# Tile 0 first: its norm, two query units and the scores of head 0 move into the merge block, and the choice of head 0 opens the expert block

## What is computed

```
merged = gates[:, :, 0, :] * conv_out + gates[:, :, 1, :] * attn_out
x = x + merged @ w_out[l]
h2 = rmsnorm(x, norm2_g[l])
x = x + peer_ffn(h2, peer_w_query[l], peer_sub_keys[l], peer_u[l], peer_v[l])

def peer_ffn(...):          # per token, for 8 heads
    q = (hc @ w_query)      # 8 heads x 2 halves x 128
    sc = einsum('thpd,pnd->thpn', q, sub_keys)      # 2 x 128 scores
    vals, idx = top_k(sc, 16)                       # 16 best of each half
    top_s, pos = top_k(cand, 16)                    # 16 best of their 256 sums
    gate = softmax(top_s)
    act = gelu(einsum('thkd,td->thk', expert_u[expert_idx], hc))
    return einsum('thk,thkd->td', gate * act, expert_v[expert_idx])
```

## Time and profile before

| what | value |
|---|---|
| median of 3 runs | 2574.63 us (2572.73 to 2579.84) |
| profiled execution, its own time | 2570.52 us |
| its span in the trace | 2568.7 us |
| mean granted PE clock | 0.976 of full speed |
| PE busy | 2220.0 us, 86% of the span |
| DVE busy | 1697.4 us, 66% |
| ACT busy | 866.9 us, 34% |
| POOL busy | 857.3 us, 33% |
| gathers (software queue) | 536.90 MB |
| plain transfers | 143.49 MB |

### The profile page before, as it was taken

One profiled execution on the slowest core, in us unless ns is written; L12 is line 12 of the kernel. 1 busy time (PEld: TensorE's weight loads), 2 busy tenths in 40 slices (PEclk: granted clock), 3 DMA queues, 4 the chain that ended last, 5 costly groups with the idle time before them and its releaser, 6 DMA issues. The chain is left out here.

```text
span 2568.7 us, 33318 instructions
## 1 busy us (share of the span) xinstructions
PE 2220.0 (86%) x11942; PEld 1394.2 (54%) x11942; DVE 1697.4 (66%) x3855; ACT 866.9 (34%) x1931; POOL 857.3 (33%) x649
## 2 busy tenths in 40 slices
PE   8998999889987788877777777777789999999999
PEld 7886667765442334333232222322267788776787
DVE  7998797347776778666776667667544644456553
ACT  4222762333232333322232223322234223246431
POOL 0001213355454355434434343333333211212243
PEclk9999999999999999999999999999999999989999
DMA  4232215279999999999999999999942212232253
GB/s 155 101 109 95 79 50 181 74 264 412 420 421 419 421 417 409 415 420 416 418 415 416 420 416 416 410 407 420 422 172 90 87 65 72 97 128 87 91 193 107
DMA packets 131075, 682.51 MB, mean 266 GB/s; under 512 B 13536, under 2 KB 23136, under 8 KB 65120
## 3 DMA queue, kind: packets, MB, share of 16 engines
q0 software_dynamic: 73728, 536.90, 50.6%
q1 hardware_dynamic: 57184, 143.49, 16.0%
HBM read 655.70 MB, written 24.64 MB: 265 GB/s over the span
## 5 line engine op out<-in xcount | busy, mean ns | idle before, releaser
L1681 PE MATMUL bank<-peer_uv,peer_diag 128*128 128x512 f32 x2048 | 967.3, 617 | 287.6 <-ACT peer_diag L1336 277.7
L1574 DVE SCALAR_TENSOR_TENSOR peer_uv<-peer_uv,early_h 128x1024 f32<-128x1024 f32 x512 | 644.5, 1270 | 381.3 <-DMA peer_uv<-in_peer_uv,peer_index 373.7
L1681 PEld LDWEIGHTS bank<-peer_uv,peer_diag 128*128 128x128 f32 x2048 | 383.3, 195 | 832.4 <-issue 828.9
L1373 POOL DMA_INDIRECT peer_uv<-in_peer_uv,peer_index x512 | 528.6, 1033 | 750.1 <-PE bank L1681 661.4
L229 POOL TENSOR_TENSOR weight_low<-weight_ring,weight_high 128x1024 fp32r<-128x1024 f32 x100 | 243.7, 2437 | 639.3 <-ACT weight_high L212 639.3
L155 PE MATMUL bank<-hT_high,weight_high 128*128 128x512 f32 (+2 forms) x952 | 399.0, 419 | 10.2 <-POOL weight_low L229 4.3
L157 PE MATMUL bank<-hT_high,weight_low 128*128 128x512 f32 (+2 forms) x984 | 380.9, 387 | 1.5 <-issue 1.5
L156 PE MATMUL bank<-hT_low,weight_high 128*128 128x512 f32 (+2 forms) x952 | 371.1, 390 | 0.0
L212 ACT ACTIVATE weight_high<-weight_ring 128x1024 fp32r<-128x1024 f32 x169 | 178.6, 1058 | 458.2 <-PE bank L157 436.8
L1331 ACT ACTIVATE peer_gelu<-peer_dots 128x2 f32<-128x2 f32 x256 | 52.1, 203 | 793.3 <-DVE peer_uv L1574 789.5
L1336 ACT ACTIVATE peer_diag<-const,peer_weight 128x128 f32<-128x128 f32 x512 | 177.5, 394 | 116.9 <-DVE peer_weight L1479 109.7
(11 more groups left out here) (422 smaller groups left out, 2748.6 us busy)
## 6 DMA issues: line engine op xcount, KB each, us to landing
weight_ring<-in_weights SPq DMA_DIRECT2D x171, 512.0 KB, 3.3
z_store<-fill_stage SPq DMA_DIRECT2D x70, 256.0 KB, 2.4
peer_uv<-in_peer_uv,peer_index POOLq DMA_INDIRECT x512
merge_z<-z_store SPq DMA_DIRECT2D x8, 768.0 KB, 6.2
merge_z<-z_store SPq DMA_DIRECT2D x12, 512.0 KB, 4.8
score_store<-peer_work SPq DMA_DIRECT2D x16, 192.0 KB
peer_sc<-score_store SPq DMA_DIRECT2D x24, 128.0 KB
swz<-z_store SPq DMA_DIRECT2D x1, 2560.0 KB, 9.6
```

The source lines that it names most:

```text
L1373: pool.indirect_dma_start(uv[:, p % SLOTS], None, peer_uv, bass.IndirectOffsetOnAxis(index[:, n % 2, p % TOPK:p % TOPK + 1], 0)).then_inc( ...
L1574: nc.vector.scalar_tensor_tensor(uv[:, p % SLOTS, 0:D], uv[:, p % SLOTS, 0:D], 1.0, h2[:, t], ALU.mult, ALU.mult, accum_out=dots[:, p % TO ...
L1681: mm = nc.tensor.matmul(bank[2 * (t % 2) + c][:], diag[:, p % SLOTS], uv[:, p % SLOTS, D + c * 512:D + (c + 1) * 512], start=(p % PICKS == ...
```

## The change

In the merge block w_out's last `k` takes the tiles in the order 0, 1, 2, 3. Behind it PE turns tile 0, computes the first two query units for tile 0 alone, and scores them; ACT and DVE make tile 0's high and low parts; ACT keeps the two queries and scores in `early_sc`, which the expert block uses as `sc`. In the expert block DVE starts with the choice of head 0 and its index, ahead of the low parts of h2; the turning, parts and the first two query units are done for tiles 1 to 3 alone. `EARLY` is 4: 40 query steps (four units, their scores, and half of the fifth unit) run ahead of the loop in place of 71. The loop takes 9 steps in four groups instead of 8. The choices of the later heads form one stream (`choices`) with four pieces a group: a head's choice starts when its scores are kept, and not within a fixed head. `MEM_AT` moves from 46 to 58.

```diff
+                pe.wait_ge(normed, 1)
+                for f in range(DT):
+                    nc.tensor.transpose(turned_at(f), xn[:, 0, f * P:(f + 1) * P], ident).then_inc(turned, 1)
+                for n in range(2):
+                    ring = w.wait(pe, q0 + n)
+                    pe.wait_ge(added, 4)
+                    for k in range(DT):
+                        if n == 0:
+                            pe.wait_ge(x_low, k + 1)
+                        mm = product(nc, bank[2 + n][:, 0:P], ring[:, k], hT[:, k, first], k == 0, k == DT - 1)
+                    mm.then_inc(queried, 1)
+                for n in range(2):
+                    pe.wait_ge(query_kept, n + 1)
+                    pe.wait_ge(added, 6)
+                    nc.tensor.matmul(bank[4 + n][:, 0:P], query[:, n], subkeys[:, n], start=True, stop=True
+                                     ).then_inc(scored, 1)
...
-EARLY = 8
+EARLY = 4
...
-STEPS = 2
+def steps_before(g):
+    return 9 * g // 4
+LOWS_BEFORE = {3: 1, 4: 1, 5: 2}
...
-                for n in range(2, EARLY - 2):
-                    w.low_part(pool, nc.gpsimd, u0 + n)
-                lows = EARLY - 2
+                lows = 2
                 for g, n, q, t in groups():
...
+                def may_choose(m, g):
+                    if m >= HEADS or g < GROUPS * (m - 2):
+                        return False
+                    return g > (keep_score_groups()[2 * m + 1] if m < PH else keep_score_groups()[-1] + 2)
+
+                def choices():
+                    for m in range(1, HEADS):
+                        while not may_choose(m, at[0]):
+                            yield
+                        yield from choose(m)
+                        while at[0] < GROUPS * (m - 1):
+                            yield
+                        publish(m)
+                        yield
+
+                for _ in choose(0):
+                    pass
+                publish(0)
                 for n, f in enumerate(TURN_ORDER):
                     dve.wait_ge(x_high, n + 1)
...
-                for _ in both(0):
-                    pass
                 dve.wait_ge(gained, TT)
+                at = [-1]
+                ahead = choices()
```

More of the change, by code:

```diff
@@ L955, in merge_first, with turned_at @@
             "ready", "warm_ready", "added", "squared", "mean_ready", "root_ready", "rstd_ready", "normed"))
-        u0 = first_unit("wo")
+        query = st.sb("query", [P, 2, P])
+        turned, x_high, x_low, queried, query_kept, scored = (st.sem(n) for n in (
+            "turned", "x_high", "x_low", "queried", "query_kept", "scored"))
+        u0, q0 = first_unit("wo"), first_unit("query")
         tiles = z_store.rearrange("(b f) p t -> f p b t", b=3)
+        first = slice(0, P)
+        def turned_at(f):
+            return bank[f // 4][:, f % 4 * P:(f % 4 + 1) * P]
         order = (2, 3, 0, 1)
@@ L982, in _ @@
                     pe.wait_ge(low_ready, k + 1)
-                    for t in order:
+                    for t in order if k < DT - 1 else range(TT):
                         for e in range(2):
@@ L1059, in _ @@
                 mean(0)
+                scale(0)
                 add(2)
-                scale(0)
                 mean(1)
                 add(3)
-                for i in range(1, TT):
-                    scale(i)
-                    if i + 1 < TT:
-                        mean(i + 1)
+                for f in range(DT):
+                    dve.wait_ge(x_high, f // 4 * 4 + 4)
+                    nc.vector.scalar_tensor_tensor(hT.low[:, f, first].bitcast(F32R), turned_at(f), norm2[:, f:f + 1],
+                                                   hT.high[:, f, first], ALU.mult, ALU.subtract).then_inc(x_low, 1)
+                for t in range(1, TT):
+                    scale(t)
+                    if t + 1 < TT:
+                        mean(t + 1)
 HEADS = TT * PH
@@ new lines, in score @@
+                def score(n):
+                    pe.wait_ge(query_kept, n + 1)
+                    if 2 <= n < 4:
+                        pe.wait_ge(score_kept, n - 1)
+                    elif n >= 4:
+                        pe.wait_ge(first_kept, n - 3)
+                    for t in range(1 if n < 2 else 0, TT):
+                        mm = nc.tensor.matmul(bank[6 + n % 2][:, t * P:(t + 1) * P], queryT[:, n % 2, t * P:(t + 1) * P],
+                                              subkeys[:, n % 2], start=True, stop=True)
+                    mm.then_inc(scored, 1)
@@ new lines, in queries @@
+                def queries():
+                    for n in range(QUERIES):
+                        ring = w.wait(pe, u0 + n)
+                        if n >= 2:
+                            pe.wait_ge(query_kept, n - 1)
+                        for i, k in enumerate(TURN_ORDER):
+                            if n == 0:
+                                pe.wait_ge(x_low, i + 1)
+                            if n and i == DT // 2:
+                                score(n - 1)
+                                yield
+                            mm = product(nc, bank[4 + n % 2][:, tokens(n)], ring[:, k], h2T[:, k, tokens(n)], i == 0, i == DT - 1)
+                            if i == DT - 1:
+                                mm.then_inc(w.done, 1)
@@ L1670, in _ @@
                 side = queries()
-                for _ in range(DT * EARLY + EARLY - 1):
+                for _ in range(PREFIX):
                     next(side)
@@ L1684, in _ @@
                     mm.then_inc(summed, 1)
-                    for _ in range(STEPS):
+                    for _ in range(steps_before(g), steps_before(g + 1)):
                         next(side, None)
```

192 lines of the change are left out of this document (94 added, 98 removed).

## The result

The changed kernel takes 2595.34 us (median of 5 runs, 2593.06 to 2598.49), the kernel before 2574.63: ratio 1.0078, 95% interval 1.0062 to 1.0094. It is 20.7 us slower, where I forecast 2573. The profiled execution is the median one: its own time 2595.34, its span 2593.5 us, 24.8 longer than the profiled one of before.

A forecast was written before the change was run, and what follows sets the result against it. The prediction took the gathers' transfers to bound the expert loop from its first gather on. Its terms, -26.0 + 6.0 + 5.2 + 5.0 + 8.5 = -1.3 us, applied to the median 2574.63, gave 2573, range 2559 to 2585.

The forecast's parts named there:

- A: From the merge block to the first gather: it goes out earlier, at 512.9 instead of 538.93, -26.0 us.
- B: From the first to the eleventh gather: the way gets longer, 40.7 us instead of 34.7, +6.0 us.
- C: Expert loop: loads of units 4 to 7 and their stored scores now lie among the gathers, +5.2 us.
- D: Expert loop, head 1: its index comes late, behind six groups instead of three, leaving transfers idle, +5.0 us.
- E: Expert loop, heads 2 to 6: their indices come late, 1.7 us lost five times, +8.5 us.
- the lead stays: Rival for the loop's late indices: they cost nothing at heads 2 to 6, 3.3 us at head 1; 2563, chance 0.33.
- costs twice: Rival for the loop's late indices: heads 2 to 6 lose 3.5 us each, head 1 6.8; 2584, chance 0.16.
- At no cost ... The later memory product: Expert loop: the later memory product fits into about 1.5 us a group free on PE, costing nothing.
- The sum's silent term: Behind the expert loop: everything was taken as unchanged, with no term in the sum.

The follow-up runs named there:

- e9: e6 with POOL's low parts of units 2 and 3 made before the third and fourth pairs of gathers: 2565.27 us.
- e12: e9 with the load of unit 5 ahead of the first score store on SP's queue: 2564.11 us.
- e11: e6 with the load of unit 5 ahead of the first score store on SP's queue: 2566.98 us.
- e5: The changed kernel with score loads ahead of the weight load and six choice pieces a group for tile 0's groups: 2568.05 us.
- e6: e5 with 80 more idle matmuls in the groups from 150 on: 2564.75 us.
- e13: e12 with ACT keeping the last score ahead of the loop behind group 0's diagonals: 2561.70 us.
- e14: e6 with ACT keeping the last score ahead of the loop behind group 0's diagonals: 2562.05 us.
- e1: The changed kernel with the loads of later heads' scores ahead of the weight load on SP's queue: 2582.99 us.
- e2: The changed kernel with six choice pieces a group instead of four for tile 0's groups: 2576.93 us.
- e3: The kernel before with 48 more idle matmuls in the groups from 150 on: 2582.11 us.
- e4: The changed kernel with 80 more idle matmuls in the groups from 150 on: 2585.24 us.
- e7: The kernel before with 128 more idle matmuls in the groups from 150 on: 2575.82 us.
- e8: The kernel before with 80 more idle matmuls in the groups from 150 on: 2574.88 us.

## Why the prediction was wrong, by its steps

Sizes are those of the profiled executions: 24.8 us longer is -24.5 (first gather) + 34.1 (loop) + 15.2 (rest).

**A, the first gather: -24.5, predicted -26.0.** The choice took 7.84 where I had 7.8; it began 1.4 us late (506.09, not 504.7). But this is the good case. In the twelve profiled kernels with the change in it the first gather goes out between 514.1 and 521.4. In e9, at 518.9, PE had the granted clock 0.50 from 506 to 514, the lower level of 1.2 GHz, and ACT waited 3.29 us for the second query where it was 0.85; PE had been partly idle just before (2.21 of 4 us busy in 498 to 502). But e12 had the same (2.22 of 4) and kept 0.98 of the clock in 506 to 514, so what decides it is open. The order of work makes PE wait for tile 0's norm and parts in short pieces, and then run the new product at half speed in some executions. I had that idling in B, not in A.

**B, the way to the eleventh gather: +8.5, predicted +6.0.** The size is near by luck in part, for the path was another. The wait for the load of unit 4, 1.8 us in my working, did not come: I had given that load 14.1 us, and it took 8.4. Two waits came that I had at nothing. PE's third unit ended 21.8 us behind the first gather (536.2) and not 18.8: POOL issued six gathers ahead of its low part, and PE's idle time and the lower clock behind it made that unit 3.7 us longer, of which 3.0 are left, as the two units before had ended 0.7 sooner than in my working. From there to the gather it took 1.3 us more than my working has without its 1.8, and 1.1 of them are the store's. So 3.0 - 1.8 + 1.3 = 2.5 too little. By the Trainium skill, "DMA: Bandwidth & Descriptors", section on queues, rings and completion order, an engine goes round between its queues by packets; by that these transfers would not wait for the gathers' backlog. Here the two loads and the store took 8.4, 15.0 and 9.2 us, against a median of 3.3 for a load over the whole program, and the measurement decides. The place among SP's own transfers counts as well: the load of unit 5 took 15.0 us behind a score store and 7.8 and 6.6 ahead of it (e11, e12).

**C, more bytes: +5.2.** Not measured apart. In e5 and e6, where the other losses of the loop are gone, the loop is 14.0 and 12.7 us longer than before and the way 9.3 and 6.7 of it: 4.7 to 6.0 are left, which agrees. In e13 and e14 more is left, 9.1 and 7.7, and why is open.

**D and E, late indices: predicted 5.0 + 8.5 = 13.5.** Right in kind and place: waits at heads 1 to 7, gaps of the transfers behind heads 1 to 6 and none behind head 7. Each of heads 2 to 6 lost 1.3 to 1.8 us by the windows (at 625, (1.02 - 0.72) x 5 = 1.5), predicted 1.7; head 1 lost about 2, predicted 5. Taking them away gave 10.7 us alone and 13.7 with the score loads in order (1352.5 - 1338.8). That this is near the predicted 13.5 is partly luck, for by the windows the terms come to some 9 or 10, and head 1 was put too high. Of the rivals "the lead stays" is out and "costs twice" too.

**"At no cost ... The later memory product": the first step that failed.** I costed the move of `MEM_AT` by PE's free time in the groups and did not look at what stands behind its loads in SP's queue. e1 gave 6.4 us of the loop back, e5 beside e2 9.4 (1348.2 - 1338.8). That the move is what made the score loads late is read from the 60 us in SP's queue; no run moves `MEM_AT` back alone.

**The sum's silent term: the second step that failed.** The sum took all that comes behind the loop as unchanged. It is 15.2 us longer: PE idles 9.1 us more, and the low clock takes 6.8 more. For all sixteen kernels the rest is 662.5 to 664.3 us plus idle plus low, so these two are all there is. The idle part belongs to the program: e3 makes it out of the kernel before with 48 matmuls nobody reads, 35.1 us, and e4, e6 and e7 take it away. By the Trainium skill, "Runtime: NRT & Kernel Launch", section on instruction fetch, the instructions come in blocks of 16 KiB, 256 of them. The page of the profile has 96 packets and 1.57 MB for the first instruction queue, 16.4 KB each, and 97 in every kernel with 128 more matmuls, 96 in e3 and e8. Each matmul has a weight load, so 128 make 256 instructions, one block, and the idle time does come round at 128. That a fetch is what PE waits for under "issue" is argued from this, not shown. The low part changes from kernel to kernel (8.6 to 25.7) with no order that I can see; how much of its 6.8 us the change itself causes is open. The medians suggest little: 20.7 = -24.5 + 34.1 + 9.1 + 2.0.

With the two failed steps at their measured sizes, -1.3 + 9.4 + 9.1 + 2.5 (B) + 1.5 (A) = +21.2, near the 20.7 of the medians. With the 6.4 us of e1 in place of the 9.4 it is 18.2, and the low clock is in neither sum, so that the closeness should not be read as proof.

## What to carry to other kernels

When a step is moved in time, look at every in-order queue for what stands behind its transfers: a load that waits for a slot holds the next consumer's load too, even if that data has long been there. A plain transfer issued among deep gathers can take several times its usual time, here 8.4 to 15.0 us, so what runs ahead of a loop should wait for none of them, a store's completion included. Before such a transfer is blamed for a wait, look up when it landed: here one of three had landed 6.6 us before the engine went on. And when gathers move ahead of other work on the engine that issues them, ask who waits for that work. When a change adds instructions to an unrolled program, compare the stages that it does not touch, before a gain or a loss is put down to the edit; a few idle matmuls tell.

## What the runs showed of the hardware

- PE's idle time in a stage of small matmuls depends on how many PE instructions stand ahead of it in the program: 26.0 us with none added, 35.1 with 48 matmuls, 29.8 with 80, 27.5 with 128, and 8.9 us on the median for 48.
- A 512 KB load issued among queued gathers took 8.4 us, the next one, behind a score store of 192 KB, 15.0 us, against a median of 3.3 over the program. Issued ahead of that store it took 7.8 us (e11) and 6.6 us (e12).
- Of six gathers that POOL issued in a row, the fifth took 4.28 us to issue, where the three ahead of it took 0.94 each.
- A short idle time of PE can cost more behind it than itself: group 0 took 6.69 us after 4.31 idle, with a granted clock of 0.50 in 550 to 555. It took 5.09 after 3.85 (e6), and 3.67 at the full clock after 2.50 (e13) and 0.97 (e14).
